# Two of the four projections before a gated recurrence: tokens stationary, and the value projection moved to the end

## The reference, cut to what matters

```
proj = xn @ w_in                                  # 256 x 2048 @ 2048 x 8192
q, fr, v, g = split(proj)                         # 2048 columns each, 16 heads of 128
q = silu(q) * 128 ** -0.5
f = lb + (1 - lb) * sigmoid(fr);  k = 1 - f       # forget gate
o = gated_recurrence(q, k, v, log(f))             # S_t = diag(f_t) S_(t-1) + k_t v_t^T ; o_t = S_t^T q_t
o = rms_norm(o, out_gain) * silu(g)               # output gate
h = h + o @ w_out
```

## Time and profile before

| | us |
|---|---|
| median of 3 runs | 2296.19 (2296.06 to 2297.53) |
| the profiled execution | 2296.2 |
| its span, first to last instruction | 2294.4 |
| around the span | 1.8 |
| PE busy | 2283.6 (100%) |
| PEld busy | 1914.2 (83%) |
| DVE busy | 1698.3 (74%) |
| ACT busy | 1047.0 (46%) |
| DMA queue of the weights | 72.9% of 16 engines' span |

### The profile page before, as it was taken

How to read it: one execution, slowest core, us unless ns; L and a number is a source line. 1 busy time by engine, 2 the same in 40 slices (tenths; PEclk the granted TensorE clock), 3 DMA queues, 4 the chain that set the end, 5 groups by cost and what they waited for, 6 DMA issues and landing times.

```text
span 2294.4 us, 33380 instructions
## 1 busy us (share of the span) xinstructions
PE 2283.6 (100%) x11086; PEld 1914.2 (83%) x11086; DVE 1698.3 (74%) x2135; ACT 1047.0 (46%) x1083; POOL 2.8 (0%) x9
## 2 busy tenths in 40 slices
PE   9999999999999999999999999999999999999998
PEld 8888888888888888888888888888888888888887
DVE  7979788877878888865556676766878878876554
ACT  7444444454444454444444333444444444444443
POOL 0000000000000000000000000000000000000000
PEclk9999999999999999999999999999999999999999
DMA  7555555558888888876777888667888888887754
GB/s 243 172 174 161 178 164 165 183 189 236 242 246 233 245 241 241 240 214 211 212 213 206 243 242 242 204 192 202 243 243 238 243 245 234 243 251 220 216 194 154
DMA packets 396166, 496.71 MB, mean 216 GB/s; under 512 B 18992, under 2 KB 230320, under 8 KB 395952
## 3 DMA queue, kind: packets, MB, share of 16 engines
q1 hardware_dynamic: 395072, 493.15, 72.9%
q10 hardware_dynamic: 1008, 2.43, 0.3%
HBM read 461.42 MB, written 31.98 MB: 215 GB/s over the span
## 4 chain that ended last, share of the span: by engine, by line
PE 92%; DVE 4%; issue 2%; ACT 1%; DMA 0%; DVEq 0%; SPq 0%; ACTq 0%
PE acc L1503 24%; PE acc L1501 24%; PE acc L1502 24%; PE acc L1435 11%; PE acc L1445 6%; DVE w_parts L769 1%; DVE a_diag L1095 1%; PE acc L1458 1%; DVE fpre L1080 1%; DVE kl L1062 0%; DMA raw<-in_hgrn_w_in 0%; PE side L1606 0%; PE acc L1466 0%; DVE ql L1056 0%; DVE ta L796 0%
## 5 line engine op out<-in xcount | busy, mean ns | idle before, releaser
L769 DVE TENSOR_TENSOR w_parts<-raw,w_parts 128x1024 fp32r<-128x1024 f32 x816 | 993.0, 1224 | 544.7 <-ACT w_parts L492 419.2
L492 ACT ACTIVATE w_parts<-raw 128x1024 fp32r<-128x1024 f32 x815 | 860.6, 1059 | 1065.7 <-PE acc L1503 838.5
L1501 PE MATMUL acc<-w_parts,xn 128*128 128x512 f32 x1728 | 672.9, 389 | 0.0
L1502 PE MATMUL acc<-w_parts,xn 128*128 128x512 f32 x1728 | 672.2, 389 | 0.0
L1503 PE MATMUL acc<-w_parts,xn 128*128 128x512 f32 x1728 | 672.2, 389 | 0.0
L1503 PEld LDWEIGHTS acc<-w_parts,xn 128*128 128x128 f32 x1728 | 324.3, 188 | 67.6
L1501 PEld LDWEIGHTS acc<-w_parts,xn 128*128 128x128 f32 x1728 | 324.3, 188 | 67.2
L1502 PEld LDWEIGHTS acc<-w_parts,xn 128*128 128x128 f32 x1728 | 324.3, 188 | 67.1
L1501 PE MATMUL acc<-w_parts,act 128*128 128x512 f32 x704 | 273.9, 389 | 0.0
L1502 PE MATMUL acc<-w_parts,act 128*128 128x512 f32 x704 | 273.9, 389 | 0.0
L1503 PE MATMUL acc<-w_parts,act 128*128 128x512 f32 x704 | 273.9, 389 | 0.0
(11 more groups left out here) (159 smaller groups left out, 1220.2 us busy)
## 6 DMA issues: line engine op xcount, KB each, us to landing
raw<-in_ffn_w_up SPq DMA_DIRECT2D x352, 512.0 KB, 4.5
raw<-in_ffn_w_down SPq DMA_DIRECT2D x176, 512.0 KB, 4.7
raw<-in_hgrn_w_in SPq DMA_DIRECT2D x127, 512.0 KB, 3.8
raw<-in_sc_w_in SPq DMA_DIRECT2D x96, 512.0 KB, 4.6
crossing<-turned SPq DMA_DIRECT2D x54, 512.0 KB, 3.8
moved<-crossing SPq DMA_DIRECT2D x216, 128.0 KB, 4.5
raw<-in_hgrn_w_out SPq DMA_DIRECT2D x32, 512.0 KB, 3.5
raw<-in_sc_w_out SPq DMA_DIRECT2D x32, 512.0 KB, 4.7
```

Source lines behind the costliest of these rows:

```text
L492: nc.scalar.activation(w_parts[:, c % RING, :, 0, :], raw[:, c % RING], ACT.Copy).then_inc(hi_ready, 1)
L769: v.tensor_tensor(w_parts[:, c % RING, :, 1, :], raw[:, c % RING], w_parts[:, c % RING, :, 0, :].bitcast(F32), ALU.subtract).then_inc(lo_r ...
L1501: mm(bank, x_hi, hi, start=begin and q == 0, stop=False)
L1502: low = mm(bank, x_hi, lo, start=False, stop=False)
```

## The change

F and G become token-stationary (`token_groups`), with one accumulator part of eight chunks each; Q stays as it is. The order of the groups becomes F, Q, G, V: the values come last. DVE turns F's and G's sum into `pad`, in the last step of their group and ahead of that step's split; SP stores `pad` to HBM with two transfers and fetches it into `tb` with four. DVE scales from `tb` into `pad`: F's in step 4 of Q, G's in step 5 of V; ACT's sigmoid reads `pad`, in step 5 of Q and step 6 of V. `fpre` and `kh` are made in step 6 of Q. The own product goes into `vt`, the values' buffer, and so ACT's copy of the values also waits until that product's parts are made. The first chunk of the program has its own order (`first_chunk`).

```diff
-HGRN_IN = Phase(None, 4, 4, DT, scales=3, wide_group=V_GROUP)
+F_GROUP, Q_GROUP, GATE_GROUP, V_GROUP = range(4)
+HGRN_IN = Phase(None, 4, 4, DT, scales=3, wide_group=V_GROUP, token_groups=(F_GROUP, GATE_GROUP))
+F_SCALED_AT, F_SIGMOID_AT, F_BOUND_AT = 4, 5, 6
+GATE_SCALED_AT, GATE_SIGMOID_AT = 5, 6
...
+            def store_heads(i, n):
+                sp.wait_ge(turned_ready, at(i, HGRN_IN.turns, n + 1))
+                store_pad(heads_stored)
+            def fetch_heads(i, n):
+                stored = 16 * (T // P)
+                sp.wait_ge(heads_stored, at(i, HGRN_IN.turns * stored, (n + 1) * stored))
+                fetch(moved_sums)
+            def cross_heads(i, first, g, kk):
+                if (g, kk) == (F_GROUP + 1, STORED_AT):
+                    store_heads(i, 0)
+                if (g, kk) == (F_GROUP + 2, FETCHED_AT - HGRN_IN.cpg):
+                    fetch_heads(i, 0)
+                if (g, kk) == (GATE_GROUP + 1, STORED_AT):
+                    store_heads(i, 1)
+                if not first:
+                    cross_last_head(i - 1, g, kk)
...
                 if b == 0:
+                    act_e.wait_ge(product_parts_ready, at(i, 2, 2))
                     act_e.wait_ge(first_values_done, at(i, 1, 1))
...
-                if kk == last and g != V_GROUP:
-                    scaled(i, HGRN_IN, g, min(g, V_GROUP), ta[:])
+                if (g, kk) == (F_GROUP + 1, F_SCALED_AT):
+                    scaled_moved(i, HGRN_IN, 0, scaled_heads, moved_sums)
+                if (g, kk) == (Q_GROUP, last):
+                    scaled(i, HGRN_IN, g, 1, ta[:])
+                if (g, kk) == (GATE_GROUP + 1, GATE_SCALED_AT):
+                    scaled_moved(i, HGRN_IN, 1, scaled_heads, moved_sums)
...
-                if (g, kk) == (1, 0):
+                if (g, kk) == (F_GROUP + 1, F_BOUND_AT):
...
-                    v.tensor_tensor(tb[:], qh[:], kh[:], ALU.mult).then_inc(product_ready, 1)
+                    v.tensor_tensor(own_product, qh[:], kh[:], ALU.mult).then_inc(product_ready, 1)
             def levels(i, first, g, kk):
+                if kk == last and g in HGRN_IN.token_groups:
+                    turn_group(i, HGRN_IN, g, turned_sums, HGRN_IN.token_groups.index(g))
...
-                            pe.wait_ge(acc_free, at(i, HGRN_IN.api, V_GROUP * HGRN_IN.parts + b + 1))
+                            pe.wait_ge(acc_free, at(i, HGRN_IN.api, HGRN_IN.first_part(V_GROUP) + b + 1))
...
+            def first_chunk(to, src):
+                w = w_parts[:, 0]
+                products = [(n, x, y) for n in range(KC) for x, y in ((0, 0), (1, 0))] + [(n, 0, 1) for n in range(KC)]
+                for n, x, y in products:
+                    if (n, x, y) == (1, 0, 0):
+                        pe.wait_ge(hi_ready, 1)
+                    if (n, x, y) == (0, 0, 1):
+                        pe.wait_ge(lo_ready, 1 + RING)
...
```

More of the change, by code:

```diff
@@ L71, in __init__, with first_part, corrected_before, by_tokens @@
         assert self.cpi % RING == 0 and self.c0 % RING == 0 and self.api % SETS == 0
+    def first_part(self, g):
+        return sum(1 if n in self.token_groups else self.parts for n in range(g))
+    def corrected_before(self, g):
+        return self.parts * sum(not self.wide(n) for n in range(g))
+    def by_tokens(self, g):
+        return self.parts == 1 or g in self.token_groups
     def wide(self, g):
-        return self.parts == 1 or g == self.wide_group
+        return self.by_tokens(g) or g == self.wide_group
     def steps(self, first, g):
@@ L82, in steps @@
             order = [(0, 0), (0, 1), (1, 0), (1, 1), (0, 2), (1, 2), (0, 3), (1, 3)]
-        elif first and g == 0 and self is HGRN_IN:
-            order = [(0, 0), (1, 0), (0, 1), (1, 1), (0, 2), (0, 3), (1, 2), (1, 3)]
         elif first and g == 0 and self.cpg == 8:
@@ L496, in correction @@
                 act_e.wait_ge(lo_used, at(i, phase.cpi, c + 1 + RING))
-                a = g * phase.parts + part
+                a = phase.first_part(g) + part
                 act_e.wait_ge(acc_free, at(i, phase.api, phase.a0 + a + SETS))
@@ L524, in body @@
                                 values(i, 1, c)
-                            elif ends and phase.corrections:
+                            elif ends and phase.corrections and not phase.wide(g):
                                 correction(i, phase, g, part, c)
@@ L747, in body @@
                                 ahead(i, first, g, kk)
-                            early = first and phase is HGRN_IN and g == 0
-                            if early and ends:
-                                corrected(i, phase, g, part, into(g))
                             if not last:
                                 split(i, phase, c + RING)
-                            if ends and phase.corrections and not early and g != phase.wide_group:
+                            if ends and phase.corrections and not phase.wide(g):
                                 corrected(i, phase, g, part, into(g))
@@ L791, in corrected @@
             def corrected(i, phase, g, part, dst):
-                a = g * phase.parts + part
-                skipped = phase.parts if phase.wide_group is not None and g > phase.wide_group else 0
-                dve.wait_ge(corr_ready, at(i, phase.corrections, phase.corr0 + a - skipped + 1))
+                a = phase.first_part(g) + part
+                dve.wait_ge(corr_ready, at(i, phase.corrections, phase.corr0 + phase.corrected_before(g) + part + 1))
                 v.tensor_tensor(dst[:, part * TW:(part + 1) * TW, :], acc[:, a % SETS, :, 0:T], corr[:], ALU.add) \
@@ L1549, in body @@
                                 c = phase.c0 + g * phase.cpg + kk
-                                a = g * phase.parts + part
+                                a = phase.first_part(g) + part
                                 if begin:
                                     pe.wait_ge(acc_free, at(i, phase.api, phase.a0 + a + 1))
-                                need = k + 1 if phase.parts == 2 else k * KC // TG + 1
+                                need = k * KC // TG + 1 if phase.by_tokens(g) else k + 1
                                 halves = first and c == 0
```

108 lines of the change are left out of this document (60 added, 48 removed).

## The result

| kernel | median of the runs, us | lowest to highest | ratio, 95% interval |
|---|---|---|---|
| before | 2296.28 | 2296.06 to 2297.53 (4 runs) | |
| changed | 2318.52 | 2317.51 to 2319.3 (4 runs) | 1.0095, 1.0083 to 1.0108 |

The changed kernel is 22.2 us slower; 17.4 had been forecast. The profiled execution took 2319.3 us with a span of 2317.4, against 2294.4 before: 23.0 more. The phase behind the recurrence, the output projection HGRN_OUT, starts at 426.15 instead of 404.80, so 21.3 of the 23.0 us are lost ahead of it. The other 1.7 are lost in its first matmuls, and nothing behind them.

A forecast was written before the change was run, and what follows sets the result against it. PE was taken to bound the kernel, with DVE full beside the third and fourth group. Iteration 0 adds 3.4 us, iterations 1 to 3 add 14.0: + 17.4 on 2296.2 gives 2313.6, own range 2309 to 2318, wide 2303 to 2320.

The forecast's parts named there:

- `qh` 2.02 later: In iteration 1, behind the moved `fpre` and `kh`, `qh` starts at 161.90, 2.02 us later, with DVE's rows behind it.
- First wait: At the product stage behind the third group's fourth chunk, PE waits 1.0 us for DVE's `pair_parts`.
- Second wait: In V's first pair, ahead of block 1, PE waits 2.1 to 2.5 us for DVE's transposes of G's sum.
- Third and fourth wait: Last level stage waits for DVE's take, 209.9 to about 210.8; F's start waits for ACT's values copy, until 212.0.
- An iteration, + 4.7: Each of iterations 1 to 3 grows 4.7 us net: F starts 5.2 later, less 0.52 from its matmul pitch.
- No idle time of DVE beside G and V: Sign in the third and fourth group: the forecast is wrong if DVE shows idle time there.
- The start, - 1.8: Iteration 0's third group starts at 53.7, not 55.55, 1.8 us earlier; no change taken up to chunk 4.
- rival 4: Idle PE falls to 1.2 GHz; a chunk costs 2.7 us more, once per iteration: + 11, time 2324; chance 0.03.
- The transfers: Storing and fetching F's and G's sums, 3.8 and 4.5 us per group, fit their room; no cost taken.
- The pitch: A token-stationary pair of chunks takes 5.44 us against 5.57, so F wins 0.52 us per iteration.

The follow-up runs named there:

- all edits with the earlier fetch: Changed kernel with F's scaling, sigmoid and `fpre`/`kh` earlier, G's scaling and sigmoid later, F's sum fetched one weight load earlier: 2297.02 us, ratio 1.0003.

## Why the prediction was right, point by point

The way and the path were right; the size was a little short. The measured 2318.5 lies at the upper edge of the forecast's own range (2309 to 2318) and inside the wide one (2303 to 2320).

- **`qh` 2.02 later: right.** 6.7 us behind the third group's start, forecast 6.7. The third group starts at 158.04, not 155.22; with this 2.82 added, the forecast puts `qh` at 164.72, the transposes at 186.87 and G's scaling at 210.85. They started at 164.73, 186.88 and 211.19. The delay alone, put into the kernel before, cost 1.96 us per iteration.
- **First wait, 1.0: right.** 0.98 of idle, in iterations 1 to 3. In iteration 0 it was 2.54; the sum had taken the same 5.2 for every iteration.
- **Second wait, 2.1 to 2.5: right.** 2.12, by the distance of V's matmuls. It had no price of its own in this kernel: with level 3's operands behind the turn it was gone and nothing was won. The prediction did not add the four waits up. It carried DVE's list to the end of V, went on over ACT's copy, and took F's start from there, and that is the path which the experiments bear out.
- **Third and fourth wait: right.** 1.14 of idle, forecast 0.9 (210.8 - 209.9), and 0.99, forecast 1.2. F starts 57.2 us behind the third group, forecast 212.0 - 155.22 = 56.8.
- **An iteration, + 4.7: 5.1 measured** (104.04 from F's start at 111.20 to that at 215.24, against 98.97 before), but + 6.5 in the two behind it (105.5), which have the lower clock at F's start.
- **No idle time of DVE beside G and V: nearly so.** In G it is the 1.13 us ahead of `qh`, as before; in V it is 0.45 behind the turn, which the sum left out (G's scaling came 0.34 later than forecast), and the 1.43 behind the last take.
- **The start, - 1.8: - 3.0 measured,** by the third group's first matmul (52.50 against 55.55). From chunk 4 to there it is 34.07 us where it was 35.83: - 1.8, as forecast. The rest lies ahead of chunk 4, where the forecast took no change:

```profile
18.43 0.39 PE L1552 MATMUL acc<-w_parts,xn 128*128 128x512 f32 x1
```

  Before, chunk 4 began at 19.72, behind 0.65 us of idle. DVE now makes its tokens from 16.55 on instead of 18.00, and PE does not wait for them. In the kernel with F alone and the earlier fetch chunk 4 begins at 18.63; so its 2.83 us ahead of the first product stage are 1.1 ahead of chunk 4 and 1.8 behind it. Iteration 0 behind the start lost 6.4 where 5.2 stood in the sum, so both errors nearly cancelled: 3.3 against 3.4. That this part fits is luck.
- **The mis-sized term: the clock,** rival 4, to which 0.03 was given and no part of the forecast. Its mechanism came on top of the forecast, not instead of it. At F's start in iterations 2 and 3 (from 215.24 and 320.73) the first seven or so 512-column matmuls stand 0.43 us apart instead of 0.23, and so do HGRN_OUT's first ones (from 426.15). They cost 1.4, 1.6 and 1.7 us, 4.7 in all, a fifth of the loss. The fourth stretch stands behind the turn's wait in iteration 0:

```profile
66.11 0.74 PE L1702 MATMUL side<-pair_parts,sum_ones 128*128 128x512 f32 x2 [2.54 <-DVE pair_parts L1118]
...
111.20 0.49 PE L1552 MATMUL acc<-w_parts,xn 128*128 128x512 f32 x1 [0.80 <-ACT vt L557]
```

```profile
86.00:88.00 2.00, 2.00 (x19) 1.32 (x18) 2.00 (x4) 0.94 (x1) 0.00 (x0) 0.50 1.08 356
```

  It cost nothing. From the product stage to F's next start it is 111.20 - 66.11 = 45.09 us with it and 215.24 - 170.09 = 45.15 without it: the last take, waited for 1.14 us in iteration 1, is not waited for here. The rival's price had been a whole chunk, 2.7 us, once per iteration. The Trainium skill (TensorE: Matmul & The Clock Gate, The HAM clock gate) says that an idle array goes down to 1.2 GHz; the rows show the lower level even behind waits as short as these, though not behind each. With 17.4 + 4.7 = 22.1 and the 0.37 us by which each of three iterations was dearer than 4.7, it is 23.2 in the profiled execution, where 23.1 was measured (2319.3 - 2296.2).
- **The transfers: no cost at the step as changed, right.** F's scaling does not wait for its fetch in iterations 1 to 3, and 0.08 us in iteration 0. The fetch costs as soon as the scaling moves up: 3.5 to 4.4 us of DVE's time in the first iteration and up to 1.6 in later ones.
- **The pitch: right.** F's chunks stand 2.72 apart, and F alone won up to 0.48 us per iteration, forecast 0.52.

Summed another way, as PE's own account: its waits grew by 20.0 us. By the distance of matmuls each cost about 0.16 more than its idle time (1.14 against 0.98, 2.12 against 1.96), which over 16 waits is 2.5. The clock ahead of HGRN_OUT took 3 x 1.7; the one in iteration 0 is counted here, since it made the waits behind it shorter. The start gave 3.0, F's pitch 3 x 0.52 and G's 4 x 0.52 back. This gives 21.0 us at HGRN_OUT's start, against 21.3 measured. Such a sum says where PE's time went, and not what would come back if one term were taken away. The start differs between executions too: the product stage of iteration 0 stood at 66.11 in the changed kernel and at 68.16 in the one with G's sigmoid later, though both have the same order up to there.

## What to carry to other kernels

Before an operation is moved or added on a helper engine, read that engine's busy time in the very stretch that gets it, not over the span: DVE's 74% hid a stretch of 27.50 in 27.72 us, where each us more was a us of time. Follow the helper's list from the moved operation to the end of the loop, and the in-order queue behind it on the third engine; the waits of the bounding engine are symptoms, and one that is removed without shortening that list comes back further on. The same holds for a slower clock of the bounding engine: it costs time only where nobody else is being waited for. Do the parts of a change apart: F alone, with its fetch one place earlier, wins 4.3 us, where both groups together lost 22.

## What the runs showed of the hardware

- The granted clock went to its lower level behind short waits, but not behind each. What decides it is open. In this case's eleven traces there are 28 places in the recurrence phase where PE stood idle for 1.8 us or more (one wait, or the last take's and the copy's together). Behind 14 of them the clock is at half for about 3.4 us, and 512-column matmuls stand 0.427 us apart instead of 0.23; those are the paces of 1.2 and 2.4 GHz. The idle time does not tell the two halves apart: with F's bounding earlier, 1.10 + 0.94 us in iteration 0 were followed by it, 1.16 + 0.98 in iterations 1 and 2 not; the turn's 1.97 in iteration 3 was, its 1.98 in iteration 2 not.
- So variants of this kernel carry between none (F alone, or all edits with the earlier fetch) and four such stretches (the changed kernel). One at F's start cost 1.4 to 1.7 us. One inside the part in which DVE sets the pace cost nothing that can be seen (43.91, 44.00 and 43.97 us with it, 43.91 without). Two variants are to be compared by stretches that hold the same number of the first kind.
- The mean clock does not show it: 0.996 for the changed kernel, 0.999 before. Only the stretch does (0.92 from 215 to 237).
- A wait's idle time in the trace was 0.16 us less than what the matmuls' distance shows it to have cost.
